# Moving tile slots and weight rings to different places modulo 512 bytes in a two-block transformer kernel

## The reference

```python
for l in range(2):
    h = rms_norm(x, g_pre_mix[l]) * (1 + sc_mix) + sh_mix
    y = mixer(h, ...)                      # w_in 1024x4096, w_q, w_k, w_v, convolutions, w_out 2048x1024
    x = x + gt_mix * rms_norm(y, g_post_mix[l])
    h = rms_norm(x, g_pre_mlp[l]) * (1 + sc_mlp) + sh_mlp
    f = square(relu(h @ w_ff1[l])) @ w_ff2[l]
    x = x + gt_mlp * rms_norm(f, g_post_mlp[l])
proj = rmsnorm(x, attn_norm_w) @ w_in_2    # 1024x4168
x = x + (sigmoid(g_a) * (o_a @ w_branch_a) + sigmoid(g_b) * (o_b @ w_branch_b)) @ w_out_2
u = relu(rmsnorm(x, mlp_norm_w) @ w_up);  x = x + (u * u) @ w_down
return rmsnorm(x, final_norm_w)
```

## Time and profile before

| | us |
|---|---|
| median of 3 runs | 2536.84 (2533.47 to 2542.15) |
| the profiled execution | 2532.14 |
| its span, first to last instruction | 2530.4 |
| PE busy | 2410.5 (95%) |
| DVE, POOL, ACT busy | 1356.2, 1116.7, 963.0 |

### The profile page before, as it was taken

How to read it: one execution, slowest core, us unless ns; L and a number is a source line. 1 busy time by engine, 2 the same in 40 slices (tenths; PEclk the granted TensorE clock), 3 DMA queues, 4 the chain that set the end, 5 groups by cost and what they waited for, 6 DMA issues and landing times.

```text
span 2530.4 us, 29267 instructions
## 1 busy us (share of the span) xinstructions
PE 2410.5 (95%) x10750; PEld 1908.9 (75%) x10750; DVE 1356.2 (54%) x2070; ACT 963.0 (38%) x1526; POOL 1116.7 (44%) x554
## 2 busy tenths in 40 slices
PE   4989799999999999889999999998999999999998
PEld 4866577878888878666777888876775668788887
DVE  6889845873533799974566112265566433412222
ACT  3347443331332335754233223335533432422332
POOL 2578512534434639761263444462431014444443
PEclk7999899989999999999999999999997999999999
DMA  6522102525545423220122323322330003233232
GB/s 236 192 83 69 58 26 82 188 92 183 166 153 171 152 73 101 63 73 26 42 83 80 95 91 100 99 76 72 91 84 26 1 26 100 80 95 99 92 99 75
DMA packets 215222, 239.88 MB, mean 95 GB/s; under 512 B 9738, under 2 KB 188746, under 8 KB 215114
## 3 DMA queue, kind: packets, MB, share of 16 engines
q1 hardware_dynamic: 215114, 238.45, 29.9%
HBM read 236.32 MB, written 2.10 MB: 94 GB/s over the span
## 4 chain that ended last, share of the span: by engine, by line
PE 80%; DVE 10%; issue 2%; ACT 1%; POOL 1%; DMA 0%; DVEq 0%; SPq 0%; ACTq 0%; POOLq 0%
PE product L2245 22%; PE product L2246 21%; PE product L2247 21%; DVE side L1668 5%; PE side L2750 2%; PE product L2321 2%; PE side L2548 1%; PE product L2572 1%; PE product L2772 1%; PE side L2760 1%; PE side L2307 1%; PE side L2314 1%; PE side L2341 1%; PE side L2566 1%; PE product L2341 1%
## 5 line engine op out<-in xcount | busy, mean ns | idle before, releaser
L869 POOL TENSOR_TENSOR ring_low<-ring_f,ring_high 128x1024 fp32r<-128x1024 f32 (+1 forms) x350 | 847.3, 2426 | 1260.0 <-ACT ring_high L978 1259.8
L2245 PE MATMUL product<-slot_r,ring_high 128*128 128x512 f32 x2792 | 1107.5, 397 | 43.5 <-ACT slot_f L1162 9.8
L2246 PE MATMUL product<-slot_r,ring_low 128*128 128x512 f32 x2792 | 1094.2, 392 | 0.0
L2247 PE MATMUL product<-slot_r,ring_high 128*128 128x512 f32 x2792 | 1093.9, 392 | 0.0
L2245 PEld LDWEIGHTS product<-slot_r,ring_high 128*128 128x128 f32 x2792 | 529.0, 189 | 173.5 <-issue 32.7
L978 ACT ACTIVATE ring_high<-ring_f 128x1024 fp32r<-128x1024 f32 (+1 forms) x350 | 367.7, 1054 | 704.2 <-DMA ring_f<-in_w_ff 340.9
L2247 PEld LDWEIGHTS product<-slot_r,ring_high 128*128 128x128 f32 x2792 | 528.5, 189 | 112.6
L2246 PEld LDWEIGHTS product<-slot_r,ring_low 128*128 128x128 f32 x2792 | 529.3, 190 | 110.5 <-issue 1.7
L1634 DVE SCALAR_TENSOR_TENSOR va<-product,sqt 128x512 f32<-128x512 f32 x96 | 66.2, 691 | 354.7 <-ACT sqt L1057 353.1
L1668 DVE SCALAR_TENSOR_TENSOR side<-slot_f,cols,side 128x512 f32<-128x512 f32 x332 | 220.6, 744 | 0.0
L1647 DVE TENSOR_TENSOR slot_f<-product,slot_f 128x512 f32<-128x512 f32 x64 | 44.1, 690 | 184.2 <-PE product L2247 184.2
(11 more groups left out here) (282 smaller groups left out, 2201.4 us busy)
## 6 DMA issues: line engine op xcount, KB each, us to landing
ring_f<-in_w_ff SPq DMA_DIRECT2D x128, 512.0 KB, 3.6
slot_f<-in_w_ada SPq DMA_DIRECT2D x48, 1024.0 KB, 6.1
ring_f<-in_w_in SPq DMA_DIRECT2D x96, 512.0 KB, 3.7
ring_f<-in_w_out SPq DMA_DIRECT2D x40, 512.0 KB, 3.5
ring_f<-in_w_up SPq DMA_DIRECT2D x32, 512.0 KB, 3.7
ring_f<-in_w_down SPq DMA_DIRECT2D x32, 512.0 KB, 3.4
slot_f<-in_x SPq DMA_DIRECT2D x4, 512.0 KB, 9.1
ring_f<-in_w_v SPq DMA_DIRECT2D x4, 512.0 KB, 3.8
```

Of the source, the lines that this page charges most:

```text
L869: pool.tensor_tensor(ring_low[:, s, :, 0:n], ring_f[:, s, :, 0:n], ring_high[:, s, :, 0:n].bitcast(F32), ALU.subtract).then_inc(low_ready. ...
L2245: pe.matmul(out_ap, high, rhs_high, start=start, stop=False)
L2246: pe.matmul(out_ap, low, rhs_high, start=False, stop=False)
L2247: return pe.matmul(out_ap, high, rhs_low, start=False, stop=stop)
```

## The change

Unused columns are put between tensors, so that they start elsewhere modulo 512 bytes. Starts modulo 512, before and after:

| | before | after |
|---|---|---|
| slot 0 (SA) | 128 | 0 |
| slot 1 (SB_) | 128 | 128 |
| slot 2 (SC) | 128 | 320 |
| slot 3 (SD) | 128 | 64 |
| slot 4 (SE) | 64 | 0 |
| slots 5, 6, 7 (SF, SG, SH) | 128 | 0 |
| ring_low, ring_f | 128 | 256 |
| ring_high, X, ident, ones, cols | 128 | 0 |
| sqt, va | 384 | 256 |

```diff
-        HEAD_ROOM, ROWS_ROOM = 256, 248
+        HEAD_ROOM, B_ROOM, C_ROOM, D_ROOM, ROWS_ROOM, RING_ROOM = 352, 32, 48, 64, 104, 64
         AROW, XROW = T + CONV_C - 1, T + CONV_M - 1
-        SA, SB_, SC, SD = 0, SLOT, 2 * SLOT, 3 * SLOT
+        SA, SB_ = 0, SLOT + B_ROOM
+        SC = SB_ + SLOT + C_ROOM
+        SD = SC + SLOT + D_ROOM
         SE = SD + NT * AROW
...
+        sb("low_room", [P, RING_ROOM])
         with nc.sbuf_tensor("ring_f", [P, RING, KC, CW], F32) as ring_f:
             pass
         ring_low = sb("ring_low", [P, RING, KC, CW], F32R)
+        sb("high_room", [P, RING_ROOM])
         ring_high = sb("ring_high", [P, RING, KC, CW], F32R)
...
-                steps.did(dve.memset(region_f[:, SD:SE].rearrange("p (t c) -> p t c", t=NT)[:, :, 0:CONV_C - 1], 0.0))
+                steps.did(dve.memset(region_f[:, SD:SD + NT * AROW].rearrange("p (t c) -> p t c", t=NT)[:, :, 0:CONV_C - 1], 0.0))
```

## The result

The changed kernel takes 2573.18 us (median of 4 runs, 2553.85 to 2591.27) against 2535.15 us for the kernel before: a ratio of 1.013, with a 95% interval of 1.0075 to 1.0185. It is slower by 1.3%, beyond the 2558 us at which my range ended. The profiled execution took 2588.02 us with a span of 2586.2 us, 55.8 us more than before.

A forecast was written before the change was run, and what follows sets the result against it. The prediction took PE, chiefly its three fp32r matmuls per product, to bound the kernel. All terms summed to 0 against the profiled 2532.1 us, so it forecast a median of 2536 us, range 2466 to 2558.

The forecast's parts named there:

- The bound and the stock: PE bounds; its fp32r matmuls' excess of about 13 ns each, 110 us in all, is what addresses could give back.
- The zero terms of DVE, POOL, ACT, DMA and the plain matmuls: Outside the fp32r matmuls, moved addresses were to cost 0, with small ends of -2 and +3 us.
- PE's fp32r matmuls: I take 0: The products' matmuls: 0 taken, between 11.4 ns a matmul gained and 13.1 ns lost.
- rival B: Slower: fp32r tiles of slots 2 and 3, 64 beyond a 128-byte multiple, pay 13.3 ns a matmul; 2570 us; chance 0.22.
- Rival A: Faster: fp32r tile reads and weight loads at equal places hinder each other; freed steps give 62 us, 2475 us; chance 0.32.

The follow-up runs named there:

- e8: The kernel before with only the two rings moved, so every tile starts 192 bytes (modulo 256) beyond its weights; 2571.7 us, ratio 1.0116.
- e7: The kernel before with slots and rings moved to places different modulo 512 but equal modulo 256; 2528.6 us, ratio 0.9959.
- e2: The changed kernel with its slots left as changed and both rings at 0 modulo 512; 2574.2 us.
- e11: The changed kernel with slot 2 at 256 and slot 3 at 0 instead of 320 and 64; ratio 1.0069 to the kernel before.
- e13: The e8 kernel with every product using only the first 72 columns of its weight block; 2529.9 us.
- e14: The kernel before with every product using only the first 72 columns of its weight block; 2602.0 us.

## Why the prediction was wrong

**The bound and the stock: right.** PE's fp32r pace was where an address could cost anything, and all of the change's loss is there: none of the lines shown above moved by more than 0.6% in its median.

**The zero terms of DVE, POOL, ACT, DMA and the plain matmuls: right**, by the single lines above. The plain matmuls of 512 columns kept their 430 ns: those of the mixer's products on slot tiles start 429 to 430 ns apart in the median in all 17 traces.

**The step that failed is the term "PE's fp32r matmuls: I take 0".** Measured, it is 18 to 20 ns a product on slots 0 and 1, 6 to 7 on slots 2 and 3 and next to nothing on the others, 30 to 33 us at the end. I justified the 0 by the nearest row, the plain matmuls at odd starts. That row is of another kind: it reads each column over two passes, and shows no effect even at places where fp32r pays. I had seen that slack and named it under rival B, but did not let it move the term. My second reason, that a constant pace in every stretch speaks for a fixed cost, proved nothing, since before every tile and every weight block lay at distance 0. A trace in which a quantity never varies can't tell that it doesn't matter. Nor was the pace the same everywhere: the eight products with blocks of 72 columns took 695 ns each at distance 0, in a trace that I had.

**Rival A** looked at the right pair, the streamed tile and the weights, and had the wrong sign: equal places are the cheap case. The rule of the Trainium skill that I weighed against it (TensorE: Matmul & The Clock Gate, Part 2, "Step-by-step: what each phase is for"), that loading weights takes no bandwidth from the running matmul, does not carry here: in e8 only the place of the weights changed, and a product went from 681 to 700 ns in the mean.

**Rival B** had the right side, and for the wrong pair. It put 13 ns on each matmul of slots 2 and 3, 33 us; there it is 2 ns, 6 us. Slots 0 and 1, which I left free of cost, pay 20 ns a product, 28 us. That the total comes out alike is chance. Its mechanism, a tile's own boundary, fell with e8, where no tile moved. With 0.22 on slower and a range that ended at 2558, I had left this out.

**The noise** was taken too small as well: I let 7.6 us be told from no change, and the runs of the kernel before lie between 2521 and 2550 us, in two groups by their clock.

## What to carry to other kernels

With one-pass fp32r matmuls back to back, start the streamed tiles and the weight blocks at equal places modulo 256 bytes when a block is 128 columns wide; in the two kernels here that have such places throughout, before and e7, these matmuls kept 227 ns, and other distances cost 2 to 8 ns a matmul, 1.8% of this kernel in e8. With blocks of 72 columns the equal place was not the best one. A room added for another tensor can shift it, so look at the addresses after each change of layout. Before an address effect is ruled out from a trace, ask whether any row varies the distance in question for the same kind of matmul.

## What the runs showed of the hardware that I had not expected

- The place matters modulo 256 bytes, and as a distance of tile and weights: moving the rings alone (e8) costs 19 ns a product in the mean, slots and rings apart by 256 (e7) nothing.
- The cost is not graded: 64 beyond costs 6 to 7 ns a product (687), 32 and 96 cost 19 (700).
- A stretch of products keeps to one pace or one pattern, and at the same distances another stretch has another one (700, 696, 693 or 687 ns with slots 0 and 1 at 0 and 128, in e2 and e11). What chooses it is open.
- The plain float32 matmuls looked at (429 to 430 ns in all 17 traces) don't show any of this. The cause inside the chip is not shown by any run: only that the weights' place takes part (e8), and the width of their block (e13, e14).
- 226.7 ns is 13 ns more than 512 columns need. The Trainium skill (TensorE: Matmul & The Clock Gate, "Wait — 56ns, not 53.3ns?") gives 2.5 ns; none of the 17 kernels brought the fp32r step of a whole stretch below 226.
